# A two-matrix MLP by a 2x2 block scheme with seven products instead of eight

## The reference, cut

```
x = layer_norm(DN_ALPHA * x + mix, ln1_g[i], ln1_b[i])
hid = jnp.square(jax.nn.relu(x @ w_ff1[i]))
ple = jax.nn.sigmoid(x @ w_ple_gate[i]) * (p[i] @ w_ple_proj[i])
x = layer_norm(DN_ALPHA * x + hid @ w_ff2[i] + ple, ln2_g[i], ln2_b[i])
```

## Time and profile before

| | |
|---|---|
| median of three runs (lowest, highest) | 1398.57 us (1397.6, 1400.42) |
| span of the profiled execution | 1397.8 us |
| TensorE busy | 1334.7 us, 95% |
| VectorE, ScalarE, GpSimd busy | 47%, 31%, 19% |
| granted clock, mean over the span | 0.982 |
| gate | 601.5 to 691.0 us |
| ff1 and ff2, eight blocks | 691.0 to 1387.3 us |

### The profile page before, as it was taken

The page is one execution under the profiler, slowest core; times in us unless marked ns, Lnnn a source line. Parts: engine busy times, 40 slices in busy tenths (PEclk is TensorE's granted clock), DMA queues, the critical chain, the costliest instruction groups (busy, mean ns, idle before and its releaser), DMA issues.

```text
span 1397.8 us, 18138 instructions
## 1 busy us (share of the span) xinstructions
PE 1334.7 (95%) x6224; PEld 1111.7 (80%) x6224; DVE 653.9 (47%) x1430; ACT 437.4 (31%) x860; POOL 266.6 (19%) x137
## 2 busy tenths in 40 slices
PE   4999999999998989989999999999999999999996
PEld 3778878878886768868888888888888888888885
DVE  3157767767767665544232242322423224232278
ACT  3145545545555631122130220302203022030220
POOL 0212112112121112101041040411404114041120
PEclk8999999999999999989999999999999999999999
DMA  7313213113205474483021030300302003020023
GB/s 171 86 37 97 49 49 96 48 49 96 48 23 162 149 199 134 151 316 91 1 83 39 15 105 0 90 30 15 105 0 90 30 15 105 0 90 30 15 74 92
DMA packets 95936, 107.40 MB, mean 77 GB/s; under 512 B 7824, under 2 KB 76560, under 8 KB 95888
## 3 DMA queue, kind: packets, MB, share of 16 engines
q1 hardware_dynamic: 95888, 106.84, 26.2%
HBM read 81.65 MB, written 16.96 MB: 71 GB/s over the span
## 4 chain that ended last, share of the span: by engine, by line
PE 53%; DVE 3%; issue 0%; DVEq 0%; ACT 0%
PE bank L1436 25%; PE bank L1450 22%; PE bank L1417 6%; DVE y L880 1%; DVE ln_stats L859 1%; DVE y L873 1%; DVE y L1390 1%; DVE ln_mean_var L866 0%; DVE ln_mean_var L868 0%; DVE w_ff_lo L1353 0%; DVE ln_mean_var L876 0%; DVEq L1153 0%; ACT w_ff_hi L1294 0%; DVE ln_mean_var L865 0%; DVEq L864 0%
## 5 line engine op out<-in xcount | busy, mean ns | idle before, releaser
L1273 POOL TENSOR_TENSOR w_ff_lo<-weight_raw,w_ff_hi 128x1024 fp32r<-128x1024 f32 x64 | 159.3, 2509 | 605.1 <-ACT w_ff_hi L1291 605.1
L1436 PE MATMUL bank<-act_T_hi,w_ff_hi 128*128 128x512 f32 x512 | 199.2, 389 | 0.0
L1436 PE MATMUL bank<-act_T_lo,w_ff_hi 128*128 128x512 f32 x512 | 199.2, 389 | 0.0
L1436 PE MATMUL bank<-act_T_hi,w_ff_lo 128*128 128x512 f32 x512 | 199.2, 389 | 0.0
L1450 PE MATMUL bank<-w_ff_hi,hidden_T_hi 128*128 128x512 f32 x512 | 199.2, 389 | 0.0
L1450 PE MATMUL bank<-w_ff_hi,hidden_T_lo 128*128 128x512 f32 x512 | 199.2, 389 | 0.0
L1450 PE MATMUL bank<-w_ff_lo,hidden_T_hi 128*128 128x512 f32 x512 | 199.2, 389 | 0.0
L1390 DVE TENSOR_TENSOR y<-y,bank 128x512 f32<-128x512 f32 x128 | 87.8, 686 | 214.8 <-PE bank L1450 214.7
L1332 ACT ACTIVATE relu<-bank 128x512 f32<-128x512 f32 x64 | 38.3, 599 | 442.1 <-PE bank L1436 442.1
L1380 DVE TENSOR_TENSOR relu<-relu 128x512 f32<-128x512 f32 x64 | 70.2, 1098 | 192.3 <-ACT relu L1332 192.3
L729 PE MATMUL bank<-act_T_hi,w_qkv_hi 128*128 128x512 f32 x384 | 153.9, 401 | 5.6 <-DVEq L682 4.6
(11 more groups left out here) (134 smaller groups left out, 2073.1 us busy)
## 6 DMA issues: line engine op xcount, KB each, us to landing
weight_raw<-in_w_ff SPq DMA_DIRECT2D x64, 512.0 KB, 3.8
weight_raw<-in_na_w_qkv SPq DMA_DIRECT2D x24, 512.0 KB, 4.4
x_tokens<-in_x SPq DMA_DIRECT2D x8, 512.0 KB, 11.7
bias_in<-rpb_rows SPq DMA_DIRECT2D x256, 6.0 KB
...
attention_T<-out_T SPq DMA_DIRECT2D x8, 512.0 KB, 2.9
weight_raw<-in_na_w_o SPq DMA_DIRECT2D x8, 512.0 KB, 4.6
```

Of the source, the lines that this page charges most:

```text
L1273: nc.gpsimd.tensor_tensor(dst, S.raw[:, slot, :], hi.bitcast(F32), ALU.subtract).then_inc(w_lo, 1)
L1436: mm = nc.tensor.matmul(S.ps[i % 4][:, :], w1[wp][:, c % 2, k, :], S.act[ap][:, k, th * HALF:(th + 1) * HALF], start=(k == 0 and n == 0), ...
```

## The change

Both products of the MLP are cut in two-by-two blocks and done with seven block products instead of eight (a Strassen scheme with shared sums, Winograd's form). The blocks of sums are themselves split in high and low parts. What is different:

- **x**: GpSimd makes four combinations of the quarters of `x` (`x_combinations`) in the gate stage, from high plus low; they are split again into `xc`.
- **w_ff1**: 16 units of 256 hidden columns (1 MB loads). Per unit GpSimd makes four sums of 128x512, ScalarE and VectorE split seven operands (`w1_high`, `w1_low`), one unit ahead (`ahead`).
- **ff1**: seven products of 12 matmuls per unit in the order `UNIT_STEPS`. Products 1 and 2 share a bank, 6, 7 and 4 share one, 5 and 3 share one: a partial sum stays in PSUM and the next product goes on adding to it, after VectorE or ScalarE has read the sum so far. VectorE makes five sums from banks (`plus`); ScalarE does relu and square; VectorE makes four sums of squared blocks (`hidden_sum`).
- **hidden values** go to DRAM: seven operands of 256 KB per unit, read back by 1 MB (`load_hidden`).
- **ff2**: four cubes of seven steps; a step is one product for four token tiles of 12 matmuls. GpSimd makes four sums of 128x2048 per cube; per step ScalarE and VectorE split one 128x2048 weight operand and four 128x512 hidden operands; VectorE adds four banks.
- **y** is no longer in SBUF during gate and ff1: the gate stage stores it to DRAM (`y0`), and it is loaded over the place of `act_T` when ff1 is over (`load_y`, 4 x 1 MB). Every add of ff2 into `y` waits for all four loads.
- **end**: GpSimd adds the shared sum to three quarters of `y` (12 instructions of 128x512), and adds the layer norm's shift (8 of 128x1024). Normalisation is in the loop of the last two steps.
- the loops are written out in full.

The core of the diff:

```diff
+UNIT_STEPS = (1, 4, 5, 6, 2, 7, 3)
+PREP = (1, 5, 6, 2, 7, 4, 3)
...
+PRODUCTS = (1, 2, 5, 3, 6, 7, 4)
+STEPS2 = len(PRODUCTS) * CUBES
...
+CONTINUES = {2: 1, 3: 5, 4: 7}
...
+            for n in range(STEPS2):
+                b, i = divmod(n, len(PRODUCTS))
+                if n + 2 < STEPS2:
+                    load_hidden(n + 2)
+                if n == 0:
+                    load_w2(0, A12)
+                    load_y(A11)
+                    load_w2(0, A22)
+                    for q in (A22, A12, A21):
+                        load_y(q)
...
+            def sums_2_4(u):
+                pool.wait_ge(s_lo, 7 * u + 2)
+                sub(columns(w_sum_tile[:, :]), columns(w_sum_tile[:, :]), w1_raw(u, A11), w_sum)
+                pool.wait_ge(w_sum, 4 * u + 3)
+                pool.wait_ge(s_lo, 7 * u + 4)
+                sub(w1_raw(u, A12), w1_raw(u, A12), columns(w_sum_tile[:, :]), w_sum)
...
+            for q, n in ((A12, n6), (A21, n6), (A22, n6 + 1)):
+                for t in range(PAIR_TILES):
+                    pool.wait_ge(added, done2(n, t))
+                    nc.gpsimd.tensor_tensor(y_block(q, t), y_block(q, t), shared_sum[:, t, :], ALU.add).then_inc(merged, 1)
+            pool.wait_ge(ln_in, 32)
+            for t in range(GROUPS):
+                pool.wait_ge(scaled, t + 1)
+                nc.gpsimd.tensor_tensor(y[:, t, :], y[:, t, :], shift[:, :], ALU.add).then_inc(out_ready, 1)
...
+                if n == 0:
+                    act.wait_ge(full[4], LAST_UNIT)
...
+                if mine:
+                    ahead(u + 1, 1)
+                    dve.wait_ge(full[5], u + 1)
+                    dve.wait_ge(p1_copied, u + 1)
...
+                    plus(stage[:, A22, :], bank_c(u), first_product[:, u % 2, :], e5_done)
+                if u:
+                    dve.wait_ge(hs_done, in_units(before + 1, HS1))
+                    hidden_sum(before, HS2, HS1, A11, ALU.subtract)
...
+                if mine:
+                    ahead(u + 1, 2)
+                    dve.wait_ge(full[6], u + 1)
...
+                    plus(stage[:, A21, :], bank_b(u), first_product[:, u % 2, :], u2_done)
+                    ahead(u + 1, 3)
+                    ahead(u + 1, 4)
...
+                elif p == 7:
+                    bank = bank_b(u)
+                    pe.wait_ge(u2_done, u + 1)
...
+            for n in range(STEPS2):
+                if n + 1 < STEPS2:
+                    w2_low(n + 1)
+                for t in range(PAIR_TILES):
+                    if n + 1 < STEPS2:
+                        hid_low(n + 1, t)
+                    add_product(n, t)
+                    if n >= STEPS2 - 2:
+                        normalise(t + PAIR_TILES * (n == STEPS2 - 1))
```

More of the change, by code:

```diff
@@ new lines, in mlp, with in_units, wb_slot, early_slot @@
+        BLOCK_ORDER = (A11, A22, A21, A12)
+        SUM_ORDER = (HS1, HS3, HS2, HS4)
+        def in_units(units, q):
+            order = BLOCK_ORDER if q in BLOCK_ORDER else SUM_ORDER
+            return 4 * (units - 1) + order.index(q) + 1
+        def wb_slot(part, w):
+            return wb[:, part, w // 2, (w % 2) * HALF:(w % 2 + 1) * HALF]
+        def early_slot(part, i):
+            return early[:, i, part, :]
+        def columns(a):
+            return a.rearrange("p (k n) -> p k n", k=KH4)
@@ L1296, in _ @@
+            nc.scalar.activation(wb_slot(0, 1), S.raw[:, 0, HALF:D], ACT.Copy).then_inc(w_hi, 1)
             for i in range(1, 4):
[L1297 to L1304 removed]
@@ new lines, in _ @@
+            for u in range(UNITS1):
+                between(u, True)
+                ahead(u + 1, 2)
+                ahead(u + 1, 3)
+                act.wait_ge(full[2], u + 1)
+                if u:
+                    act.wait_ge(hid_stored[A11], 16 * u)
+                    act.wait_ge(hs_done, in_units(u, HS2))
+                    act.wait_ge(hs_done, in_units(u, HS3))
+                else:
+                    act.wait_ge(gate_done, GATE_TILES)
+                nc.scalar.activation(stage[:, A11, :], bank_a(u), ACT.Relu).then_inc(relu_done, 1)
+                ahead(u + 1, 4)
+                square(u, A11)
+                relu(u, A22, c22_done)
+                ahead(u + 1, 5)
+                square(u, A22)
+                ahead(u + 1, 6)
@@ L1338, in _ @@
+            between(UNITS1, False)
+            for n in range(1, STEPS2):
+                w2_high(n)
+                for t in range(PAIR_TILES):
+                    hid_high(n, t)
             for t in range(GROUPS):
@@ L1402, in _, with plus, hidden_sum @@
-            blocks_loop(dve, body)
+                if u < GATE_TILES - 1:
+                    x_low(u)
+                if u == GATE_TILES - 2:
+                    x_low(u + 1)
+                if u == GATE_TILES - 4:
+                    w1_low(0, 0)
+            for i in range(1, 6):
+                w1_low(0, i)
+            def plus(dst, bank, other, count):
+                nc.vector.tensor_tensor(dst, bank, other, ALU.add).then_inc(count, 1)
+            def hidden_sum(u, dst, a, b, op):
+                if u:
+                    dve.wait_ge(hid_stored[dst], 16 * u)
+                nc.vector.tensor_tensor(stage[:, dst, :], stage[:, a, :], stage[:, b, :], op).then_inc(hs_done, 1)
```

774 lines of the change are left out of this document (586 added, 188 removed).

## The result

| | before | after |
|---|---|---|
| median of 4 runs | 1399.14 us (1397.6 to 1400.42) | 1368.26 us (1364.38 to 1368.84) |
| ratio | | 0.9773 [0.9759, 0.9787] |
| profiled span | 1397.8 us | 1366.6 us |
| the gate stage begins at | 601.46 | 603.06 |
| gate | 89.5 | 92.7 |

2.3% faster; the forecast was 1348 us, so 20 us of the forecast gain are missing. The stage rows go from the first matmul of one stage to the first of the next, and ff2's to the end of its last matmul. (Before, the gate's 89.5 us run to the end of its last matmul; the first of ff1 starts 0.16 earlier.) 7/8 of 696.3 would be 304.6 us for each of ff1 and ff2: the edges cost ff1 13.1 us and ff2 17.6.

The account below looks back on a forecast made before the run. Matmuls on TensorE were taken to bound the kernel. From the 1397.8 us span, 87.0 came off and 1.0, 5.0, 2.4, 1.5 and 26.3 were added: 1347.0, as a median 1348 us; range 1326 to 1372.

Parts of the forecast that it names:

- matmuls bound, edges paid: Whole kernel: matmuls set the time and stage edges cost extra; chance 0.60, by itself 1338 to 1360 us.
- the lock: VectorE instructions with both inputs in SBUF wait for the GpSimd instruction under way; those with an input in PSUM don't.
- 384 matmuls at 226.7 ns: ff1 and ff2 together: 2688 matmuls instead of 3072, saving 87.0 us at most.
- gate: Gate stage: its added copies on VectorE, ScalarE and GpSimd lie under matmuls and cost nothing.
- unit 0 and unit 15: First and last units of ff1: late low parts and sums make TensorE wait, 5.0 and 2.4 us.
- ff2, steady: ff2's steps: a cube's last two GpSimd sums back to back leave low parts at most level with TensorE; 1.0 us.
- seam: From ff1 to ff2: queued loads bring y late, and step 2's second low part comes late for TensorE; 1.5 us.
- TensorE in the last two steps: End of ff2: late low parts among normalisations; TensorE ends 25.5 us after step 26's start instead of 21.76.
- behind the last matmul: After TensorE's last matmul: 33 us of VectorE and GpSimd, where before the change 10.5 us followed.
- the lock rival: Steady ff1 and ff2: with all collisions units take 1.5 us longer, steps 0.5; 36 us more, 1384; chance 0.17.
- Steady ff1: A steady ff1 unit: the tight place is product 7, with slack of 1.2 us, so no stall.
- The end, 26.3 us: Last two steps to the final store: late low parts, normalisations and GpSimd's colliding shifts lose 26.3 us.

Follow-up runs that it names:

- e4: The changed kernel with second weight quarters, hidden 2 and y for ff2 loaded ahead of the last unit's stores; median 1363.8 us, ratio 0.9742 to before.
- e1: The changed kernel with GpSimd's x combinations held until the first half of the gate's weights is split; median 1361.8 us, ratio 0.9728 to before.
- e5: The changed kernel with low parts in units 0 and 15 moved later in VectorE's list, in unit 15 on ScalarE too; median 1359.7 us, ratio 0.9722.
- e6: The changed kernel with the first cube's later GpSimd weight sums held until step 2's hidden operands are split; median 1369.9 us, ratio 0.9791 to before.
- e10: The changed kernel with each GpSimd sum of 128x2048 in ff2 cut in four of 128x512; median 1360.4 us, ratio 0.9717 to before.
- e2: The changed kernel with the last step's four hidden low parts ahead of step 26's adds and normalisations; median 1365.9 us, ratio 0.9766 to before.
- e12: The changed kernel with e1, e4, e5, e10, step 26's normalisations behind its adds, and the layer norm's shift on VectorE; median 1345.8 us, ratio 0.9611.

## Why the prediction was right, and where its sum was off

The forecast's mechanism held: matmuls bound, edges paid. 1368 lies inside the range (1326 to 1372), but above the 1338 to 1360 that the forecast alone would have had. That the range held is in part luck: its upper part was there for the lock in the steady state, which did not come; other costs filled it. In the profiled spans 1366.6 stands against 1347.0:

| term | forecast | measured | of it waits |
|---|---|---|---|
| 384 matmuls at 226.7 ns | -87.0 | -87.0 | |
| start of the gate stage | 0 | 1.6 | |
| gate | 0 | 3.2 | 0.8 |
| unit 0 and unit 15 | 5.0 + 2.4 | 13.1 | 8.0 |
| ff2, steady | 1.0 | 0 | |
| seam | 1.5 | 12.9 | 8.5 |
| TensorE in the last two steps | 3.7 | 4.7 | 2.3 |
| behind the last matmul | 22.6 | 20.3 | |
| sum | -50.8 | -31.2 | |

1. **The clock behind the waits was left out of the sum.** "after 3.16 us idle the nine matmuls from 601.46 to 605.43 took 0.44 us each", "some 2 us each time", stands in the forecast only in the lock rival. It belonged to every wait that the forecast had itself found. It is the largest thing left out: 14.3 us of TensorE's 33.9 (gate 2.4, ff1 5.1, seam 4.4, end 2.4). At the end it costs nothing, as VectorE sets the pace there: in e4 the matmuls behind the same wait of 1.87 us ran at the full rate (3.04 us for twelve instead of 4.43), and TensorE then waited 1.85 us instead of 0.46 for VectorE. e1 and e5 show it from the other side, by gaining more than the waits that they took away.
2. **The seam's term, 1.5 us, was mis-sized.** The step considered the loads and VectorE's order, and put the lock's cost elsewhere ("In ff2 the worst are the last two GpSimd sums of a cube back to back"). Its own figures don't give 1.5 either: step 2's second tile is due at 21.4 + 21.8 + 2.7 = 45.9 on unit 15's clock, not at 48.7, so its low part at 50.2 would be 4.3 late. Measured on that clock (zero at 990.10), `y` was there at 52.6, not 48.7, and VectorE ready for it at 51.7, not 45.6. What the step lacked is cube 0's sums: they can't begin until their quarters land, so the first holds up step 2's weight part (3.1 us of wait, e6), and the others collide with the low parts that are due then (the rest of the 8.5 us). e10 shows the collisions: the same sums in pieces, up to 4.3 us back. The queue took 25.6 us from 1017.0 to `y`, against 21 forecast. The rate was near the forecast's (381 GB/s against 395), but that is 9.8 MB where 7.3 were counted. e4, which queues the loads earlier, gets 4.3 us back and leaves 6.3 of waits.
3. **The gate, "at nothing", cost 3.2 us.** The cover named, matmuls, exists in the gate's middle, and there the cost is next to nothing (TensorE busy 78.8 of 79 us from 612 to 691). At its first tiles TensorE waits for VectorE, and GpSimd's new sums make VectorE wait. e1 shows it.
4. **Unit 0 and unit 15 were right in their waits**: 0.97 + 4.56 against 0.5 + 4.5, 2.45 against 2.4. Steady ff1 too: margin 1.45 us against the forecast's 1.2. The 1.0 us of steady ff2 was not needed; TensorE never waits from 1060 to 1300, with VectorE busy 194.4 of 240 us, collisions included.
5. **The end, 26.3 us, came out at 25.0**, by a partly different route. The forecast let TensorE wait for low parts; what it waits for is the add of step 26, whose bank product 7's successor continues. e2 shows that: low parts first, and the waits remain. The shift's backlog, eight in a row to the end, lasted only four shifts; from 1344.7 on VectorE set the pace. The multiplication by a column took 0.75 us, as the slope gave (0.76), and 2.64 when it met a shift.

Where the gain went, then: of the 87.0 us of matmuls, 20.3 went back behind the last matmul because the last two steps now end all eight tiles, 33.9 to the edges of the stages, 1.6 to the later start. e12 gets back 21 of the 33.9 (gate 1.1, ff1 and ff2 5.9 each are left), 12.4 of them waits and the rest the clock behind them.

Of the later start of the gate stage (1.6 us) about 0.5 is its very first low part, 1.16 us for 0.69. The rest stays open: the start varies over 4.1 us between these runs, though only e1's edit touches anything ahead of it.
